# Rotary parts of queries and keys in a hybrid decoder layer: transposed on TensorE instead of by block transposes and placing DMAs

## The chip, the core and the metric

One core of a Trainium2 chip runs the whole layer. The metric is device time in microseconds, the median of several runs of one kernel. The engines are TensorE (PE, matrix products, results go to PSUM), VectorE (DVE), ScalarE (ACT), GpSimd (POOL) and SyncE (SP, which here issues nearly all DMAs). They run their own queues in program order and meet by semaphores.

## The reference, cut to what matters

```python
h = x @ w_in[l]                       # 512 tokens, 1024 wide
(qa, ka, va, ga, iq, ik, iw, c_q, c_kv, k_rope, gb) = _split_cols(h)
...
o_a = _dsa_branch(qa, ka, va, iq, ik, iw) * jax.nn.silu(ga)      # branch A: top-128 of the keys
# branch B: latent attention, 8 heads of 64 + 32
q = (_rmsnorm(c_q, q_norm_g) @ w_uq).reshape(B, S, B_HEADS, B_NOPE_DIM + B_ROPE_DIM)
q_nope, q_pe = q[..., :B_NOPE_DIM], _rope(q[..., B_NOPE_DIM:], pos)
k_pe = _rope(k_rope[:, :, None, :], pos)[:, :, 0, :]             # one key part for all heads
s = (einsum('bthd,bshd->bhts', qn, k_nope) + einsum('bthr,bsr->bhts', qp, k_pe)) * scale
...
out = jnp.concatenate([o_a, o_b], axis=-1) @ w_out[l]
x = _layernorm(DEEPNORM_ALPHA * x + out, ln_g[l], ln_b[l])
```

## The kernel before

All of it is one straight program. PE first multiplies x by the columns of w_in (groups of 512 columns, three products each for the high and low halves of the numbers), until about 159 us. Then come the small products of branch B: `qpe_tok` (the rotary part of the queries, tokens on partitions, 4 tiles of 128 tokens by 8 heads x 32), the 64-wide parts of `qbT` and `kbT` (head dimension on partitions, 512 tokens on the free axis), and `vb`. After these runs a loop over 64 units `u`: 8 heads for each of four query tiles of 128 tokens, branch A for u = 0 to 31 and branch B for u = 32 to 63. Query tiles are taken from the last, so the number of keys is 512 for u = 0 to 7, 384 for 8 to 15, then 256 and 128, and the same again for branch B.

In step u, PE computes the scores of u (L1310 and L1313, for branch B L1320), the transposes of the probabilities of u - 2 (L1355, `T_LAG`), and the value products of u - 4 (L1371, `PV_LAG`). DVE masks the scores and takes the row minimum (L951). ACT copies the transposed probabilities of u - 2 out of PSUM (L708) and computes the exponential of u (L688). At u = 12 and 13 DVE also normalises (L967, L968) and gates (L977) the first query tile. POOL, beside the loop, splits w_out into high and low parts (L511, L515): four of its eight row blocks come by `w_raw`, the others by `wo_early` and then `wo_raw_b`. After step 18 PE transposes a gated tile (L1400), and ACT copies it over the place where `wo_early` was, once all high parts of w_out are made.

The scores of branch B need `qbT` and `kbT` with all 96 rows: 64 rows by PE, and 32 rotary rows (partitions 64 to 95) that have to be turned from tokens on partitions to features on partitions. POOL rotates `qpe_tok` (L489 to L493, until about 172 us), DVE the key part `kpe_tok` (long before). Before the change the turning is done in two parts. DVE transposes blocks of 32x32 within their place: `kpe_blk` (L880) once, `qpe_blk` in four pieces (`qpe_blocks`, L939) at u = 3 to 6 (`PET_AT = 3`). Then SP issues four DMAs for each, one for each group of 32 partitions (`place`, L386), which carry the blocks, 32 elements at a stretch, to rows 64 to 95 of `kbT` (head 0) and of `qbT`. One more DMA (L403) copies the key rows of head 0 to the other seven heads.

SP works its list in order: the kaT_swap copies (L381, needed by the first scores, L1313), the four key placements, three loads of w_out to `w_raw` (L365), the key broadcast, two `wo_early` loads, a wait for `qpe_blocked`, the load of w_out block 0 (it goes to the place where `qpe_tok` lies), the four query placements, two more `wo_early` loads (each waits for a cast on POOL), and then a wait for the scores of u = 31 ahead of `wo_raw_b`. In front of unit 32, PE waits for `kpe_copied` and `qpe_placed`.

PSUM has 8 banks of 512 f32 columns. Banks 0 to 3 (`acc`) hold the products ahead of the loop; in the loop banks 2 and 3 are `ps_y`, idle until the output products at u = 34. `acc_ready` counts fills of these banks in order, `acc_read[i]` counts by twos what was read of bank i.

Of the kernel before, what the change touches and what calls it, by code (L numbers as in the profile page):

```python
# [6 lines left out]
P = 128  # L7
SEQ, D_MODEL = 512, 1024
TT = SEQ // P
# [5 lines left out]
B_HEADS, NOPE, ROPE_D, V_DIM = 8, 64, 32, 64  # L15
# [12 lines left out]
def build(nc, x, xT, positions, freqs, w_in, q_norm_g, w_uq, kv_norm_g, w_ukv, w_out, ln_g, ln_b, out):  # L28
# [93 lines left out]
    def sb(name, kib, shape, dt=f32):  # L122
        return nc.alloc_sbuf_tensor_at(name, shape, dt, offset=base + int(kib * 1024))
# [23 lines left out]
    qpe_blk = sb("qpe_blk", 94, [P, B_HEADS, TT, ROPE_D])  # L147
# [38 lines left out]
    kpe_blk = sb("kpe_blk", 204.5, [P, TT, ROPE_D])  # L186
    SQ = 32
# [23 lines left out]
    with ExitStack() as ctx:  # L211
# [14 lines left out]
        kaT_swapped, stored = sem("kaT_swapped"), sem("stored")  # L226
        kpe_blocked, qpe_blocked = sem("kpe_blocked"), sem("qpe_blocked")
        kpe_placed, kpe_copied, qpe_placed = sem("kpe_placed"), sem("kpe_copied"), sem("qpe_placed")
# [17 lines left out]
        qpe_rotated = sem("qpe_rotated")  # L246
# [33 lines left out]

        def seen(n):
            return 2 * (n // 4)
# [4 lines left out]
        ACC_LAST = [last_seen(range(A_END), b) for b in range(4)]  # L287
# [64 lines left out]
        def _(sp):  # L352
# [30 lines left out]
            def place(a, dst, blk, done):  # L383


                sp.dma_start(dst.rearrange("p h (m a t) -> p (h m) a t", a=P // SQ, t=SQ)[:, :, a, :],  # L386
                             blk[SQ * a:SQ * (a + 1)]).then_inc(done, 16)

            sp.wait_ge(kpe_blocked, 1)
            for a in range(P // SQ):  # L390
                place(a, kbT[NOPE:B_QK, 0:1, :], kpe_blk, kpe_placed)

# [9 lines left out]
            sp.wait_ge(kpe_placed, 16 * P // SQ)  # L402
            sp.dma_start(kbT[NOPE:B_QK, 1:B_HEADS, :],  # L403
                         kbT[NOPE:B_QK, 0:1, :].broadcast_to([ROPE_D, B_HEADS - 1, SEQ])).then_inc(kpe_copied, 16)
            for k in (4, 5):
                load_early(k)
            sp.wait_ge(qpe_blocked, TT)
            load(C_OUT // 2)
            for a in range(P // SQ):
                place(a, qbT[NOPE:B_QK, :, :], qpe_blk[:, :, :, :].rearrange("p h m t -> p (h m) t"), qpe_placed)  # L410
            for k in (6, 7):
                load_early(k)
# [139 lines left out]
        def _(act):  # L552
# [18 lines left out]
            def evac_group(g):  # L571
                dst = {G_IDX: idx_tok, G_LAT: lat_tok, G_Q: q_tok, G_K: k_tok, G_V: va}.get(g, gate)
                off = A_WIDTH if g == G_GB else 0
                n = GROUPS[g][1]
                if g == G_GA:

                    act.wait_ge(relu_used, (TT - 1) * IDX_HEADS)
                    act.wait_ge(kpe_blocked, 1)
                    act.wait_ge(side_ready, F_LAT + QL_T + 1)
                if g == G_LAT:  # L580
                    for m in range(TT):
                        act.wait_ge(side_ready, m + 1)
                        act.activation(dst[:, m, 0:n], side[:, m, 0:n], ACT.Copy).then_inc(side_read[m], 2)
                    return
                for m in range(TT):
                    act.wait_ge(acc_ready, TT * ACC_GROUP[g] + m + 1)
                    act.activation(dst[:, m, off:off + n], acc[:, m, 0:n],
                                   ACT.Silu if g in (G_GA, G_GB) else ACT.Copy).then_inc(acc_read[m], 2)
# [95 lines left out]
            act.activation(unused, minus_half[:, 0:1], ACT.Exp)  # L684
            def exp_unit(u):
                N = unit(u)[3]
                act.wait_ge(masked_ready, u + 1)
                act.activation(probs[:, u % NPROBS, 0:N], probs[:, u % NPROBS, 0:N], ACT.Exp, bias=neg_max[:, u % 8:u % 8 + 1],  # L688
                               scale=-1.0, accum_out=row_sum[:, u:u + 1]).then_inc(probs_ready, 1)
# [53 lines left out]
            for u in range(NU + T_LAG):  # L743
# [12 lines left out]
                if 0 < i < TT and j == OT_AT + 2:  # L756
                    copy_oT_hi(i - 1, 1)
                if u == VB_EARLY:
                    vb_high(0)
# [12 lines left out]
        def _(dve):  # L772
# [101 lines left out]
            for m in range(TT):  # L874
                for j, (a, b) in enumerate(((0, Q_LORA), (Q_LORA, Q_LORA + KV_LORA))):
# [4 lines left out]
            V.transpose(kpe_blk[:, :, :].rearrange("p m t -> p (m t)"),  # L880
                        kpe_tok[:, :, :].rearrange("p m d -> p (m d)")).then_inc(kpe_blocked, 1)
# [54 lines left out]
            def qpe_blocks(m):  # L936

                dve.wait_ge(qpe_rotated, 2 * TT)
                V.transpose(qpe_blk[:, :, m, :], qpe_tok[:, m, :].rearrange("p (h d) -> p h d", d=ROPE_D)).then_inc(qpe_blocked, 1)  # L939
# [115 lines left out]
            for u in range(NU):  # L1055
# [19 lines left out]
                if PET_AT <= u < PET_AT + TT:  # L1075
                    qpe_blocks(u - PET_AT)
# [41 lines left out]
        def _(pe):  # L1118
# [178 lines left out]
            def scores(u):  # L1297
# [16 lines left out]
                else:  # L1314
                    if u == NU_A:
                        for p in range(4):
                            pe.wait_ge(acc_read[p], ACC_LAST[p])
                        pe.wait_ge(kpe_copied, 16)
                        pe.wait_ge(qpe_placed, 16 * P // SQ)
# [6 lines left out]
            for p in range(4):  # L1326
# [3 lines left out]
                                     (w_lo[:, s, cols], latT_hi[:, QL_T, :])), True, True).then_inc(acc_ready, 1)  # L1330
            for m in range(TT):
# [102 lines left out]
            for u in range(NU + PV_LAG):  # L1434
# [4 lines left out]
                if u - PV_LAG >= 0:  # L1439
                    outputs(u - PV_LAG)  # L1440
                i, j = divmod(u - NU_A, HEADS)
# [26 lines left out]
PET_AT = 3  # L1468
# [45 lines left out]
```

## Time and profile before

| | us |
|---|---|
| median of 3 runs | 302.81 |
| lowest, highest | 302.24, 303.14 |
| the profiled execution | 303.14 |
| its span in the trace | 301.3 |

Of the span, PE is busy 97%, PE's weight loads 84%, DVE 77%, POOL 57%, ACT 56%. The profile's busy time counts each instruction from start to end. PE's matmuls overlap (an instruction of 128 columns is listed with about 0.27 us, while the next starts after 0.11), so PE's pace is read from the distances of the starts, not from the durations. Idle time is listed with what ended it; idle time of an engine that others don't wait for costs nothing.

### The profile page before, as it was taken

The numbers are of one execution on the slowest core, as the hardware profiler recorded it, in microseconds if no ns is written. First come the engines' busy times: TensorE is split into PE (matmuls) and PEld (weight loads), VectorE is DVE, ScalarE is ACT, GpSimd is POOL, SyncE is SP. The second block draws the span as 40 slices with busy tenths as digits, with TensorE's granted clock in tenths as the row PEclk, the third lists the DMA queues.
The fourth block names the chain that finished last, engine by engine and source line by source line (L and its number), as shares of the span: only waits on it lengthen the run. The fifth ranks groups of instructions, "written<-read, shape, count | busy, mean of one in ns | idle before, by whom it ended". The sixth has DMA issues, their size and how long they took to land.

```text
span 301.3 us, 5146 instructions
## 1 busy us (share of the span) xinstructions
PE 292.1 (97%) x1634; PEld 251.9 (84%) x1634; DVE 230.9 (77%) x525; ACT 167.4 (56%) x405; POOL 171.3 (57%) x197
## 2 busy tenths in 40 slices
PE   8899999999999999999999999999999999999990
PEld 8899988888888888888888789999677788888890
DVE  2798987878999999997043653664998868977785
ACT  4764444585152262374358787788877786553200
POOL 5698957302999995635326788530494261817211
PEclk9999999999999999999999999999999999999997
DMA  7965552200244425320055577300950000030411
GB/s 238 324 185 166 156 163 71 70 2 0 76 136 139 138 77 141 100 70 2 0 139 147 215 197 175 110 2 23 347 191 0 2 0 2 36 107 0 141 70 70
DMA packets 19546, 31.84 MB, mean 106 GB/s; under 512 B 6496, under 2 KB 9056, under 8 KB 19520
## 3 DMA queue, kind: packets, MB, share of 16 engines
q1 hardware_dynamic: 19088, 31.35, 34.5%
q8 instruction: 13, 0.21, 0.3%
q10 hardware_dynamic: 432, 0.18, 0.3%
q14 instruction: 13, 0.11, 0.1%
HBM read 26.28 MB, written 2.10 MB: 94 GB/s over the span
## 4 chain that ended last, share of the span: by engine, by line
PE 93%; DMA 2%; DVE 2%; ACT 1%; issue 1%; SPq 0%; DVEq 0%; ACTq 0%
PE ps L1124 49%; PE ps L1427 15%; PE ps L1355 6%; PE ps L1371 5%; PE ps L1320 5%; PE ps L1386 3%; PE ps L1310 2%; DMA w_raw<-in_w_in 2%; PE ps L1313 2%; PE ps L1221 1%; PE ps L1139 1%; PE ps L1240 1%; PE ps L1400 1%; PE ps L1211 1%; DVE y_last L1038 0%
## 5 line engine op out<-in xcount | busy, mean ns | idle before, releaser
L470 POOL TENSOR_TENSOR w_lo<-w_raw,w_hi 128x512 fp32r<-128x512 f32 (+3 forms) x62 | 81.1, 1332 | 32.1 <-ACT w_hi L569 32.0
L1124 PE MATMUL ps<-w_hi,x_lo 128*128 128x512 f32 (+2 forms) x224 | 82.5, 371 | 0.0
L1124 PE MATMUL ps<-w_lo,x_hi 128*128 128x512 f32 (+2 forms) x224 | 82.5, 371 | 0.0
L569 ACT ACTIVATE w_hi<-w_raw 128x512 fp32r<-128x512 f32 (+3 forms) x62 | 35.9, 590 | 71.2 <-PE ps L1124 63.1
L1124 PE MATMUL ps<-w_hi,x_hi 128*128 128x512 f32 (+1 forms) x188 | 73.1, 389 | 0.0
L1124 PEld LDWEIGHTS ps<-w_hi,x_lo 128*128 128x128 f32 x224 | 42.1, 188 | 6.4
L1124 PEld LDWEIGHTS ps<-w_lo,x_hi 128*128 128x128 f32 x224 | 42.2, 188 | 5.9
L1427 PE MATMUL ps<-wo_hi,oT 128*128 128x512 f32 (+1 forms) x144 | 43.5, 372 | 0.0
L1124 PEld LDWEIGHTS ps<-w_hi,x_hi 128*128 128x128 f32 x188 | 35.3, 188 | 5.9
L688 ACT ACTIVATE probs<-probs,small 128x512 f32<-128x512 f32 (+3 forms) x64 | 35.7, 558 | 7.6 <-DVE small L951 7.1
L1355 PE MATMUL ps<-ident,probs 128*128 128x128 f32 x160 | 28.3, 274 | 0.4 <-ACT probs L688 0.2
L1427 PEld LDWEIGHTS ps<-wo_hi,oT 128*128 128x128 f32 x144 | 25.7, 189 | 3.3
L1355 PEld LDWEIGHTS ps<-ident,probs 128*128 128x128 f32 x160 | 20.1, 140 | 9.6 <-issue 5.0
L328 POOL TENSOR_TENSOR obT<-half_sum,crossed 64x128 f32<-64x128 f32 x30 | 15.7, 523 | 17.8 <-ACT crossed L741 16.0
L908 DVE MATCH_REPLACE8 score<-small,score 128x256 f32<-128x256 f32 (+2 forms) x48 | 25.6, 548 | 0.0
L951 DVE CUSTOM_DVE_ANT_0 probs<-ps,score 128x512 f32<-128x512 f32 (+2 forms) x24 | 13.3, 556 | 15.1 <-PE ps L1313 15.1
L905 DVE MAX8 small<-score 128x8 f32<-128x256 f32 (+2 forms) x48 | 23.6, 550 | 0.0
L951 DVE CUSTOM_DVE_ANT_0 probs<-ps,causal 128x128 f32<-128x128 f32 (+3 forms) x40 | 17.7, 444 | 6.8 <-PE ps L1313 3.3
L1320 PE MATMUL ps<-kbT,qbT 96*128 96x512 f32 (+3 forms) x64 | 22.7, 435 | 0.0
L1371 PE MATMUL ps<-va,probsT 128*128 128x64 f32 x160 | 21.4, 264 | 0.0
L1371 PEld LDWEIGHTS ps<-va,probsT 128*128 128x128 f32 x160 | 20.5, 193 | 0.6 <-issue 0.6
L982 DVE TENSOR_TENSOR probsT_b<-ps,probsT_b 128x512 fp32r<-128x512 f32 (+3 forms) x32 | 15.6, 488 | 5.0 <-ACT probsT_b L708 4.6
(161 smaller groups left out, 555.7 us busy)
## 6 DMA issues: line engine op xcount, KB each, us to landing
w_raw<-in_w_in SPq DMA_DIRECT2D x20, 512.0 KB, 3.6
kaT_swap<-kaT SPq DMA_DIRECT2D x8, 256.0 KB, 3.7
w_raw<-in_w_out SPq DMA_DIRECT2D x4, 512.0 KB, 4.0
wo_early<-in_w_out SPq DMA_DIRECT2D x4, 512.0 KB, 5.4
wo_raw_b<-in_w_out SPq DMA_DIRECT2D x4, 512.0 KB, 5.2
x_res<-in_x SPq DMA_DIRECT2D x4, 512.0 KB, 7.4
x_raw<-in_xT SPq DMA_DIRECT2D x3, 512.0 KB, 7.9
out_y<-y SPq DMA_DIRECT2D x6, 256.0 KB, 2.2
```

Of the source, the lines that this page charges most:

```text
L328: eng.tensor_tensor(obT[rows, g % 4], half_sum[rows, g % 2, a], crossed[rows, g % 2], ALU.add).then_inc(pair_merged, 1)
L470: pool.tensor_tensor(w_lo[:, s, 0:n], w_raw[:, s, 0:n], w_hi[:, s, 0:n], ALU.subtract).then_inc(w_lo_ready, 1)
L569: act.activation(dst, w_raw[:, s, 0:n], ACT.Copy).then_inc(w_hi_ready, 1)
L688: act.activation(probs[:, u % NPROBS, 0:N], probs[:, u % NPROBS, 0:N], ACT.Exp, bias=neg_max[:, u % 8:u % 8 + 1], scale=-1.0, accum_out=ro ...
L905: step(V.max(top8[:, 8 * j:8 * j + 8], sc))
L908: step(V.match_replace(out=sc, in_to_replace=top8[:, 8 * j:8 * j + 8], in_values=sc, imm_value=TAKEN))
L951: V.tensor_tensor_reduce(out=probs[:, u % NPROBS, 0:N], in0=ps_s[:, u % 2, 0:N], in1=bias, scale=-scale, scalar=3.0e38, op0=ALU.add, op1=A ...
L1124: ins = mm(dst, a, b, start=start and j == 0, stop=stop and j == len(pairs) - 1)
L1320: ins = mm(ps_s[:, b, 0:N], qbT[:, h, t], kbT[:, h, 0:N], start=True, stop=True)
L1355: ins = nc.tensor.transpose(bank[:, j * P:(j + 1) * P], probs[:, u % NPROBS, j * P:(j + 1) * P], ident[:, :])
L1371: ins = mm(ps_o[:, v % 2, h * A_DIM:(h + 1) * A_DIM], probsT[:, u % 3, j * P:(j + 1) * P], va[:, j, h * A_DIM:(h + 1) * A_DIM], start=(j = ...
L1427: ins = mm(out_ps(i, b), oT[i % 2][:, o, k, :], w[:, wcols], start=first, stop=final)
```

## The change

The block transposes and the placing DMAs are taken out. PE transposes `qpe_tok` against the identity into the two banks `ps_y`: `qpe_transposes`, eight transposes, two groups of four heads, at the end of step u = 8 (`PET_AT` is now 8). The result has 128 partitions, 4 heads x 32, and 512 tokens. Four pieces of 32 partitions of each kind are then copied to rows 64 to 95 of `qbT`: heads 0, 1, 4, 5 by ACT and heads 2, 3, 6, 7 by DVE, one piece on each engine in each of the steps u = 9 to 12. At the end of u = 14 PE transposes `kpe_tok` (four transposes with 32 result partitions, `kpe_transposes`) into bank 2, and ACT copies it to `kbT`, head 0, at u = 15. The broadcast to the other heads stays a DMA, now last in SP's list before the wait for u = 31. In the diff the first `evac_qpeT` is ACT's, the second DVE's. The load of w_out block 0 waits until PE's second group of query transposes is done, instead of for DVE's.

```diff
-            for a in range(P // SQ):
-                place(a, kbT[NOPE:B_QK, 0:1, :], kpe_blk, kpe_placed)
...
             sp.wait_ge(acc_ready, A_END)
-            sp.wait_ge(kpe_placed, 16 * P // SQ)
+            for k in (4, 5):
+                load_early(k)
+            sp.wait_ge(acc_ready, A_END + 2)
+            load(C_OUT // 2)
+            for k in (6, 7):
+                load_early(k)
+            sp.wait_ge(acc_read[2], ACC_LAST[2])
             sp.dma_start(kbT[NOPE:B_QK, 1:B_HEADS, :],
                          kbT[NOPE:B_QK, 0:1, :].broadcast_to([ROPE_D, B_HEADS - 1, SEQ])).then_inc(kpe_copied, 16)
-            for k in (4, 5):
-                load_early(k)
-            sp.wait_ge(qpe_blocked, TT)
-            load(C_OUT // 2)
-            for a in range(P // SQ):
-                place(a, qbT[NOPE:B_QK, :, :], qpe_blk[:, :, :, :].rearrange("p h m t -> p (h m) t"), qpe_placed)
-            for k in (6, 7):
-                load_early(k)
...
+            def evac_qpeT(j):
+
+                quad, r = divmod(j, 2)
+                act.wait_ge(acc_ready, A_END + quad + 1)
+                ins = act.activation(qbT[NOPE:B_QK, 4 * quad + r, :], ps_y[32 * r:32 * r + 32, quad], ACT.Copy)
+                if r == 1:
+                    ins.then_inc(acc_read[2 + quad], 1)
...
+                if 0 <= u - PET_AT - 1 < 4:
+                    evac_qpeT(u - PET_AT - 1)
+                if u == PET_AT + 7:
+                    act.wait_ge(acc_ready, A_END + 3)
+                    act.activation(kbT[NOPE:B_QK, 0, :], ps_y[0:ROPE_D, 0], ACT.Copy).then_inc(acc_read[2], 2)
...
-            V.transpose(kpe_blk[:, :, :].rearrange("p m t -> p (m t)"),
-                        kpe_tok[:, :, :].rearrange("p m d -> p (m d)")).then_inc(kpe_blocked, 1)
+            dve.sem_inc(kpe_rotated, 1)
...
-            def qpe_blocks(m):
-
-                dve.wait_ge(qpe_rotated, 2 * TT)
-                V.transpose(qpe_blk[:, :, m, :], qpe_tok[:, m, :].rearrange("p (h d) -> p h d", d=ROPE_D)).then_inc(qpe_blocked, 1)
+            def evac_qpeT(j):
+
+                quad, r = divmod(j, 2)
+                dve.wait_ge(acc_ready, A_END + quad + 1)
+                ins = V.tensor_copy(qbT[NOPE:B_QK, 4 * quad + 2 + r, :], ps_y[64 + 32 * r:96 + 32 * r, quad])
+                if r == 1:
+                    ins.then_inc(acc_read[2 + quad], 1)
...
-                        pe.wait_ge(qpe_placed, 16 * P // SQ)
...
+            def qpe_transposes():
+
+                pe.wait_ge(qpe_rotated, 2 * TT)
+                for quad in range(2):
+                    pe.wait_ge(acc_read[2 + quad], seen(A_QPET + quad))
+                    for m in range(TT):
+                        ins = nc.tensor.transpose(ps_y[:, quad, m * P:(m + 1) * P], qpe_tok[:, m, quad * P:(quad + 1) * P], ident[:, :])
+                    ins.then_inc(acc_ready, 1)
+
+            def kpe_transposes():
+                pe.wait_ge(kpe_rotated, 1)
+                pe.wait_ge(acc_read[2], seen(A_KPET))
+                for m in range(TT):
+                    ins = nc.tensor.transpose(ps_y[0:ROPE_D, 0, m * P:(m + 1) * P], kpe_tok[:, m, :], ident[:, :])
+                ins.then_inc(acc_ready, 1)
...
+                if u == PET_AT:
+                    qpe_transposes()
+                if u == PET_AT + 6:
+                    kpe_transposes()
...
-PET_AT = 3
+PET_AT = 8
```

On PE, between the value products of step 8 and the scores of step 9, `ps<-kaT,qaT` are scores and `ps<-va,probsT` value products. Before:

```order
L1371 MATMUL ps<-va,probsT 128x64 [waits probsT_copied]
L1371 MATMUL ps<-va,probsT 128x64 x3
L1310 MATMUL ps<-kaT,qaT 128x384 [waits masked_ready]
L1313 MATMUL ps<-kaT_swap,qaT 128x384
L1355 MATMUL ps<-ident,probs 128x128 [waits probs_ready,probsT_copied]
```

and with the change (line numbers are those of the changed file):

```order
L1387 MATMUL ps<-va,probsT 128x64 [waits probsT_copied]
L1387 MATMUL ps<-va,probsT 128x64 x3
L1338 MATMUL ps<-ident,qpe_tok 128x128 [waits acc_read2,qpe_rotated]
L1338 MATMUL ps<-ident,qpe_tok 128x128 x3
L1338 MATMUL ps<-ident,qpe_tok 128x128 [waits acc_read3]
L1338 MATMUL ps<-ident,qpe_tok 128x128 x3
L1312 MATMUL ps<-kaT,qaT 128x384 [waits masked_ready]
L1315 MATMUL ps<-kaT_swap,qaT 128x384
```

Eight transposes stand between the two steps; four more (`ps<-ident,kpe_tok 32x128`) stand in the same way behind step 14. Nothing else of PE's order moves.

On DVE, around step 12, `probs,small<-ps,score` is the mask and `o_norm` the normalised tile of branch A. Before:

```order
L951 ISA probs,small<-ps,score 128x384 [waits transposed,scores_ready]
L951 ISA small 128x1
L967 RECIPROCAL small<-small 128x8 [waits pv_done]
L968 TENSOR_TENSOR o_norm<-ps,small 128x512 [waits dve_step]
L951 ISA probs,small<-ps,score 128x384 [waits transposed,scores_ready]
```

and with the change:

```order
L953 ISA probs,small<-ps,score 128x384 [waits transposed,scores_ready]
L953 ISA small 128x1
L969 RECIPROCAL small<-small 128x8 [waits pv_done]
L970 TENSOR_TENSOR o_norm<-ps,small 128x512 [waits dve_step]
L938 COPY qbT<-ps 32x512 [waits acc_ready]
L953 ISA probs,small<-ps,score 128x384 [waits transposed,scores_ready]
```

The fourth of DVE's copies stands behind the normalisation of step 12 and ahead of the mask of step 13.

On SP, after the kaT_swap copies, before:

```order
L386 DMA kbT<-kpe_blk 32x4x32 [waits kpe_blocked]
L386 DMA kbT<-kpe_blk 32x4x32 x3
L365 DMA w_raw<-in_w_out 128x1024 [waits w_lo_ready] x3
L403 DMA kbT<-kbT 32x7x512 [waits kpe_placed,acc_ready]
L397 DMA wo_early<-in_w_out 128x1024 x2
L365 DMA w_raw<-in_w_out 128x1024 [waits w_lo_ready,qpe_blocked]
L386 DMA qbT<-qpe_blk 32x32x32 x4
L397 DMA wo_early<-in_w_out 128x1024 [waits wo_hi_ready] x2
L415 DMA wo_raw_b<-in_w_out 128x1024 [waits scores_ready]
```

and with the change:

```order
L362 DMA w_raw<-in_w_out 128x1024 [waits w_lo_ready] x3
L384 DMA wo_early<-in_w_out 128x1024 [waits acc_ready]
L384 DMA wo_early<-in_w_out 128x1024
L362 DMA w_raw<-in_w_out 128x1024 [waits w_lo_ready,acc_ready]
L384 DMA wo_early<-in_w_out 128x1024 [waits wo_hi_ready] x2
L396 DMA kbT<-kbT 32x7x512 [waits acc_read2]
L400 DMA wo_raw_b<-in_w_out 128x1024 [waits scores_ready]
```

The placements are gone, the w_out loads stand right behind the kaT_swap copies, and the broadcast of the key rows stands behind all `wo_early` loads.

## Rows read from the trace of the kernel before

**Rows 1.** The page: busy us, share of span, instructions; PE's granted clock in tenths.

```profile
PE 292.1 (97%) x1634; PEld 251.9 (84%) x1634; DVE 230.9 (77%) x525; ACT 167.4 (56%) x405; POOL 171.3 (57%) x197
...
PEclk9999999999999999999999999999999999999997
```

**Rows 2.** The page: the chain that ended last, shares by engine.

```profile
PE 93%; DMA 2%; DVE 2%; ACT 1%; issue 1%; SPq 0%; DVEq 0%; ACTq 0%
```

**Rows 3.** Waits, 173 to 209.5: engine, line waited for, total us, times, longest us.

```profile
DVE probs L951 <- PE ps L1313: 18.4, 25, 2.4
...
PEld ps L1355 <- issue: 0.5, 1, 0.5
PEld ps L1355 <- DVE oT L338: 0.3, 1, 0.3
```

**Rows 4.** PE in order of time: start us, us, what, count [idle before].

```profile
175.40 0.47 PE L1310 MATMUL ps<-kaT,qaT 128*128 128x512 f32 x1
...
177.49 0.48 PE L1310 MATMUL ps<-kaT,qaT 128*128 128x512 f32 x1
...
181.09 0.48 PE L1310 MATMUL ps<-kaT,qaT 128*128 128x512 f32 x1
...
182.07 1.00 PE L1371 MATMUL ps<-va,probsT 128*128 128x64 f32 x8
```

**Rows 5.** The chain in order of time: start us, us, what.

```profile
110.24 1.31 PE ps L1228 x12
```

**Rows 6.** PE in order of time, around the transposes of a gated tile.

```profile
198.43 0.61 PE L1400 MATMUL ps<-ident,gate 128*128 128x128 f32 x4
198.80 0.36 PE L1310 MATMUL ps<-kaT,qaT 128*128 128x256 f32 x1
```

**Rows 7.** PE in order of time, the first scores of unit 32.

```profile
209.45 1.10 PE L1320 MATMUL ps<-kbT,qbT 96*128 96x512 f32 x2
```

**Rows 8.** DVE in order of time, u = 3 to 5.

```profile
175.86 0.44 DVE L939 STREAM_TRANSPOSE qpe_blk<-qpe_tok 128x256 f32<-128x256 f32 x1
176.22 0.65 DVE L951 CUSTOM_DVE_ANT_0 probs<-ps,score 128x512 f32<-128x512 f32 x1
...
178.24 0.69 DVE L951 CUSTOM_DVE_ANT_0 probs<-ps,score 128x512 f32<-128x512 f32 x1 [0.99 <-PE ps L1313]
```

**Rows 9.** The tile qbT: duration ns min/median/max, first and last start us.

```profile
L959 DVE COPY qbT<-ps x4: 692/694/694, 163.2 to 167.3; 64x512 f32<-64x512 f32 x4
L694 ACT ACTIVATE qbT<-ps x4: 574/593/596, 163.7 to 167.3; 64x512 f32<-64x512 f32 x4
```

**Rows 10.** In order of time, steps 12 to 15, of DVE, ACT and PE.

```profile
190.75 0.69 DVE L968 TENSOR_TENSOR o_norm<-ps,small 128x512 f32<-128x512 f32 x1
...
191.71 0.49 ACT L708 ACTIVATE probsT<-ps 128x384 f32<-128x384 f32 x1 [0.27 <-PE ps L1355]
192.10 0.61 ACT L688 ACTIVATE probs<-probs,small 128x384 f32<-128x384 f32 x1
...
193.89 0.49 PE L1355 MATMUL ps<-ident,probs 128*128 128x128 f32 x3
```

**Rows 11.** SP in order of time; PE's first use of kaT_swap, and its landing.

```profile
162.27 3.89 SPq L386 DMA_DIRECT2D kbT<-kpe_blk  x4
...
181.50 3.92 SPq L386 DMA_DIRECT2D qbT<-qpe_blk  x4
...
167.34 0.39 PE L1313 MATMUL ps<-kaT_swap,qaT 128*128 128x512 f32 x1
...
DMA to landing us min/median/max: 3.1/3.7/4.5
```

**Rows 12.** POOL in order of time, its work on w_out and behind it.

```profile
190.32 1.18 POOL L511 CAST wo_hi<-wo_early 128x512 fp32r<-128x512 f32 x2 [2.87 <-DMA wo_early<-in_w_out]
...
202.46 1.39 POOL L518 TENSOR_TENSOR vb_parts<-vb,vb_parts 128x512 fp32r<-128x512 f32 x1 [4.99 <-ACT vb_parts L732]
```

**Rows 13.** The key broadcast, L403: us from issue to landing.

```profile
DMA to landing us min/median/max: 4.5/4.5/4.5
```

More of the change, by code:

```diff
@@ L146, in build @@
     tmp = sb("tmp", 94, [P, 2, BANK])
-    qpe_blk = sb("qpe_blk", 94, [P, B_HEADS, TT, ROPE_D])
     y = sb("y", 94, [P, D_MODEL])
@@ L185, in build @@
     crossed = sb("crossed", 204.5, [P, 2, P])
-    kpe_blk = sb("kpe_blk", 204.5, [P, TT, ROPE_D])
-    SQ = 32
     def wo_lo(k, half):
@@ L225, in build @@
         xres_loaded = [sem(f"xres_loaded{i}") for i in range(2)]
-        kaT_swapped, stored = sem("kaT_swapped"), sem("stored")
-        kpe_blocked, qpe_blocked = sem("kpe_blocked"), sem("qpe_blocked")
-        kpe_placed, kpe_copied, qpe_placed = sem("kpe_placed"), sem("kpe_copied"), sem("qpe_placed")
+        kaT_swapped, kpe_copied, stored = sem("kaT_swapped"), sem("kpe_copied"), sem("stored")
         const_ready = sem("const_ready")
@@ L245, in build @@
         lat_normed, lat_hi_ready = sem("lat_normed"), sem("lat_hi_ready")
-        qpe_rotated = sem("qpe_rotated")
+        kpe_rotated, qpe_rotated = sem("kpe_rotated"), sem("qpe_rotated")
         q_step, q_rotated = sem("q_step"), sem("q_rotated")
@@ L279, in build @@
         A_END = A_VB + TT
+        A_QPET, A_KPET = A_END + 2, A_END + 6
         def seen(n):
@@ L285, in last_seen @@
             return seen([n for n in fills if n % 4 == bank][-1]) + 2
-        ACC_LAST = [last_seen(range(A_END), b) for b in range(4)]
+        ACC_LAST = [last_seen([*range(A_END), A_QPET, A_QPET + 1, A_KPET], b) for b in range(4)]
         SIDE_LAST = [last_seen(range(F_END), b) for b in range(4)]
@@ L382, in _ @@
                                  kaT[A_DIM * (1 - a):A_DIM * (2 - a), h:h + 2, :].bitcast(f32)).then_inc(kaT_swapped, 16)
[L383 to L389, printed above, removed]
-            for a in range(P // SQ):
-                place(a, kbT[NOPE:B_QK, 0:1, :], kpe_blk, kpe_placed)
             def load_early(k):
@@ L577, in evac_group @@
                     act.wait_ge(relu_used, (TT - 1) * IDX_HEADS)
-                    act.wait_ge(kpe_blocked, 1)
+                    act.wait_ge(kpe_rotated, 1)
                     act.wait_ge(side_ready, F_LAT + QL_T + 1)
@@ L1074, in _ @@
                     row_sums(v - 1)
-                if PET_AT <= u < PET_AT + TT:
-                    qpe_blocks(u - PET_AT)
+                if 0 <= u - PET_AT - 1 < 4:
+                    evac_qpeT(u - PET_AT - 1)
                 if u == O_FIRST + T_LAG + 1:
```

## The prediction

> **What bounds the kernel now.** I read the share of busy time first, then the chain of work that ended last, then the waits of the stretch that the change touches, then its instructions in order of time. TensorE (PE) is busy for 292.1 of 301.3 us, the next engine, VectorE (DVE), for 77% [rows 1]. The chain agrees: 93% of it is PE's [rows 2]. What matters is the stretch of the first attention loop (units u = 0 to 31, about 174 to 209 us), because all new PE work goes there. In its list of waits the long one is DVE's for PE: 18.4 us until scores (L1313) are done; PE's own weight loads wait 0.5 us for the sequencer and 0.3 for DVE [rows 3]. The instructions in order of time show a fixed beat: the steps of u = 5 and u = 7 start at 177.49 and 181.09, twice 1.80 us apart, with PE's groups end to end [rows 4]. So here PE's time is the kernel's time, and its granted clock is full in every slice but the last [rows 1].
>
> **PE, added.** Twelve transposes: eight of the query tile at the end of step u = 8 and four of the key tile at the end of u = 14. The chain has twelve transposes of the first form (128x128 f32, against the identity) as one piece, 1.31 us for L1228, that is 0.109 us each [rows 5]. A second reading is a group of four that stands between the loop's own groups, as the new ones will: L1400 starts at 198.43 and the scores behind it at 198.80, 0.37 us for four [rows 6]. Twelve cost 3 x 0.37 = 1.11 by this and 1.31 by the other. I take 1.3, since in a run of eight only the last overlaps what follows. Nothing of PE's is removed: the waits for placed queries and copied keys stood in front of unit 32, whose first scores start at 209.45 without idle time before them [rows 7], so these waits cost nothing.
>
> **DVE and ACT.** DVE loses one block transpose early in the run and four of 0.44 us in u = 3 to 6 [rows 8]. Their cover is DVE's waiting: behind the second of them the mask of u = 5 starts at 178.24 after 0.99 us of idle time that PE's scores end, and those of u = 6 and 7 start after idle time too [rows 8]. Only the mask at 176.22 starts as a block transpose ends (175.86 + 0.44), and PE's scores for it, begun at 175.40 [rows 4], end hardly earlier. I count the removal at nothing. Added are four copies on DVE and five on ACT, 32x512 out of PSUM. The nearest rows are the 64x512 copies: 0.69 us on DVE, 0.59 on ACT [rows 9]. Whether half the partitions is cheaper no row shows; between nothing and these values I take the whole. On ACT the step of u = 12 has 0.27 us of waiting for PE [rows 10], and a 512-column copy holds the engine about 0.5 us (one of 384 columns lets the next start after 0.39, 191.71 to 192.10 [rows 10]). ACT falls behind by about 0.2 us there and catches up in the next step. On DVE the tightest place is u = 12, where the normalisation already stands, 0.69 us at 190.75 [rows 10] and 0.2 for the reciprocals ahead of it: mask 0.6, normalisation 0.9, copy 0.65 make 2.15 us in a beat of 1.35, and the mask of u = 13 comes some 0.8 us late. From there it goes to the exponential on ACT (0.6 us, at 192.10 in this trace: 0.7 with its sum) and to PE's transposes of u = 13, two steps on, at 193.89 [rows 10]: 193.89 - 192.10 - 0.7 leaves 1.1 us, and the key transposes, which stand ahead of them, add 0.4. So a lateness of 0.8 is covered. If that cover is gone, it costs up to 0.8 us.
>
> **SP and its queue.** The eight placing DMAs go. They held SP for 3.89 us from 162.27 and for 3.92 us from 181.50 [rows 11]. What is queued behind them moves: three loads of w_out from 166.2 to about 162.3, and that of k = 0 from 181.1 to about 185.5, since it now waits for PE's eight transposes. The three loads then share the queue with the end of the kaT_swap copies, whose data PE needs at 167.34; the last of these was issued by 162.27 and they land in 3.7 us, 4.5 at most [rows 11], so 0.6 us is left at worst, and what stands behind them in the same queue should not overtake them. On POOL the cast of wo_early at 190.32 waited 2.87 us for its data, behind the placing traffic. With the load of k = 0 in its place it comes about as early, and after its last w_out piece POOL idles 4.99 us, until 202.46 [rows 12], so it is done at 197.5; ACT needs the high parts, made before that, only behind L1400's group at 198.43 [rows 6]. A slip of 1 us is covered twice. The key broadcast moves from 173.9 to behind PE's key transposes: step 15's own transposes start at 193.89 [rows 10], so step 14 ends about 193.4 + 0.9 + 0.4 = 194.7, ACT copies by about 197, the DMA takes 0.6 to issue and 4.5 to land [rows 13], so 202. It is needed at 209.45 + 1.3 = 210.7: 8 us of cover. Behind it are the wo_raw_b loads, which wait for unit 31 anyway.
>
> **A rule against this.** The Trainium skill, VectorE: DVE Perf Modes, section Rules for kernel authors, calls the DVE transpose the fastest for 32x32 blocks and sends full 128x128 ones to TensorE. By it the old way is the cheap one; this trace does not contradict it, since the block transposes hid in DVE's idle time. It leaves the sum as it is: 0 for the old way, 1.3 for the new.
>
> **Sum.** Removed from the path 0, added 1.3 (PE), all else covered: the profiled execution took 303.14 us over a span of 301.3, so it would be 304.4. That execution was the slowest of the three shown; on the median of 302.81 I forecast 304.1.
>
> **Rivals.** (a) The four key transposes cost double. They write only 32 partitions, from a stationary tile of 32 columns, a form that no row of before has. An ordinary f32 product shows as two records (L1371: 8 records for the 4 products of a step) [rows 4]; if these four ran so, they would add 4 x 0.11 = 0.44, which gives 304.5. For it speaks the unusual form; against it only that all other transposes are single records. The Trainium skill, TensorEngine Tiling (Array Packing), section Restrictions, states that column tiling disables the transpose mode for FP32 input, which would make them just that. (b) The copies stall the loop at u = 12 to 14: +0.8 on top, 304.9. It decides when the mask of u = 13 is more than 1.1 us late. (c) PE's insertion fills waits of its own: the step at 175.40 takes 2.09 us for 1.80 [rows 4], and 0.3 is lost to DVE [rows 3], near 200 us. If both swallowed new work, +0.7 is left, 303.5, no change that can be measured. Against it: the first lies ahead of the new work, the second hangs on PE's own L1400. (d) Faster: the loop is in truth a round trip (scores, mask, exponential, transpose), PE's records only look dense, and taking 4 x 0.44 = 1.8 us off DVE shortens it while the transposes fill holes: 301.0. It decides if masks start where DVE gets free; in u = 4 to 7 three of four start after an idle gap, so hardly.
>
> **How the numbers follow.** Forecast (304.1) 0.62; (a) 0.15; (b) 0.07; (c) 0.12; (d) 0.04. A measurement of this kernel tells about 0.3% from no change, 0.9 us. The forecast lies 1.3 above the median, so with the spread of the three runs (302.24 to 303.14) about one in eight of its outcomes falls within 0.3%. Slower: 0.54 + 0.15 + 0.07 = 0.76; same: 0.08 + 0.12 = 0.20; faster 0.04. The range takes in (a), most of (b), the bounds of the transposes (1.1 to 1.75) and part of (c): 303.2 to 305.2.
>
> **What would show it.** PE busy up by about 1.3 us; twelve new transposes, the step of u = 8 about 0.85 us longer and that of u = 14 about 0.4; later steps of PE unchanged, the first scores of unit 32 near 210.7 with no wait for the key broadcast; the mask of u = 13 late, with no gap of PE at u = 15. The forecast is wrong if eight records stand for the key tile, if PE waits for ACT or DVE between u = 9 and 16, or if PE waits for kaT_swap near 167.

## The result and the profile after

| | before | after |
|---|---|---|
| median of the runs, us | 302.81 (5 runs) | 304.31 (5 runs) |
| lowest, highest | 302.24, 303.14 | 303.78, 304.45 |
| the profiled execution | 303.14 | 303.76 |
| its span | 301.3 | 302.0 |

The ratio is 1.0052, with an interval of 1.0040 to 1.0065: the change costs 1.5 us (1.2 to 2.0). The forecast was 304.1. Over all 14 executions on record the changed kernel took 303.76 to 305.00 us.

The two spans differ by 0.7 us only. The profiled execution of before was the slowest of its runs and that of after is below all five runs in the table, so the two spans show less of the difference than the medians do. Before anything is explained the span has to be cut at places that both kernels have. I take four: the first scores of u = 2, the first scores of unit 32, the start of SP's last store issues, and the end of the span. The first two stand in PE's list in order of time (start us, us, engine line, operation, count):

```profile
172.67 0.39 PE L1312 MATMUL ps<-kaT,qaT 128*128 128x512 f32 x1
...
209.64 1.10 PE L1321 MATMUL ps<-kbT,qbT 96*128 96x512 f32 x2
```

The same first row of the kernel before, whose second is in [rows 7]:

```profile
173.68 0.39 PE L1310 MATMUL ps<-kaT,qaT 128*128 128x512 f32 x1
```

And SP's list in order of time, its last row, before and then after:

```profile
298.00 1.31 SPq L424 DMA_DIRECT2D out_y<-y_last  x3
```

```profile
298.19 1.30 SPq L409 DMA_DIRECT2D out_y<-y_last  x3
```

| stretch | before | after | difference |
|---|---|---|---|
| start to scores of u = 2 | 173.68 | 172.67 | -1.01 |
| the loop, u = 2 to unit 32 | 35.77 | 36.97 | **+1.20** |
| unit 32 to SP's last store issues | 88.55 | 88.55 | 0.00 |
| from the end of these issues to the end of the span | 1.99 | 2.51 | **+0.52** |

(301.3 - 298.00 - 1.31 = 1.99; 302.0 - 298.19 - 1.30 = 2.51.) The sum is 0.7. The spans are printed to 0.1 us, so the last row is good to 0.1 us only; the packed trace gives 2.01 and 2.46 us, a difference of 0.45. The first stretch, ahead of all that the change touches on PE, differs from kernel to kernel: in those below it ends at 173.06 and 173.17 with the placing DMAs of before (e1, e5), at 172.95 to 173.00 without them (e2, e3, e4, e6, e9), and at 173.46 and 173.53 with tiny DMAs added to these (e8, e10). Of the 1.01 us here, 0.67 is in the first 20 us of the program, where PE is idle for 1.84 us before and 1.17 after. What stands out is that the loop has the forecast's term and the end of the program has one that nobody had on the list.

The page of the kernel after, first part (busy us, share of the span, instructions), against [rows 1]:

```profile
PE 292.9 (97%) x1646; PEld 252.9 (84%) x1646; DVE 232.2 (77%) x524; ACT 169.9 (56%) x410; POOL 172.0 (57%) x197
```

PE has exactly twelve records more. Its list in order of time shows where they stand, first the eight of the query tile and then the four of the key tile:

```profile
182.74 1.00 PE L1387 MATMUL ps<-va,probsT 128*128 128x64 f32 x8
183.58 1.04 PE L1338 MATMUL ps<-ident,qpe_tok 128*128 128x128 f32 x8
184.38 0.42 PE L1312 MATMUL ps<-kaT,qaT 128*128 128x384 f32 x1
...
193.30 0.60 PE L1345 MATMUL ps<-ident,kpe_tok 128*32 128x128 f32 x4
193.65 0.42 PE L1312 MATMUL ps<-kaT,qaT 128*128 128x384 f32 x1
193.91 0.34 PE L1315 MATMUL ps<-kaT_swap,qaT 128*128 128x384 f32 x1
194.09 0.49 PE L1371 MATMUL ps<-ident,probs 128*128 128x128 f32 x3
```

From start to start the eight take 0.80 us and the four 0.35, together 1.15 of the loop's 1.20; counted from scores to scores, the step of u = 8 is 0.83 us longer and that of u = 14 is 0.38 longer. The scores, transposes and value products behind them follow at their old distances: nothing absorbs the twelve and nothing stalls because of them. The waits of the loop (173 to 211 us: engine, line waited for, total us, times, longest us; PEld is PE's weight loads) answer to [rows 3]:

```profile
DVE probs L953 <- PE ps L1315: 17.7, 25, 2.5
...
PEld ps L1371 <- issue: 0.5, 1, 0.5
PEld ps L1371 <- DVE oT L335: 0.3, 1, 0.3
```

DVE waits 0.7 us less for PE, and PE's own waits are the old ones.

### The profile page after: what moved, and what is told of

Its sections match the earlier page's. It is cut to its first block, busy times and chain, and to the rows that moved or that the text cites. A ratio compares the mean times of both kernels' runs of the same rounds, so it can differ in the third digit from the quotient of the medians.

```text
span 302.0 us, 5169 instructions
## 1 busy us (share of the span) xinstructions
PE 292.9 (97%) x1646; PEld 252.9 (84%) x1646; DVE 232.2 (77%) x524; ACT 169.9 (56%) x410; POOL 172.0 (57%) x197
## 4 chain that ended last, share of the span: by engine, by line
PE 93%; DVE 2%; DMA 2%; ACT 1%; issue 1%; SPq 0%; DVEq 0%; ACTq 0%
PE ps L1126 49%; PE ps L1443 15%; PE ps L1371 6%; PE ps L1387 5%; PE ps L1321 5%; PE ps L1402 3%; PE ps L1312 2%; PE ps L1315 2%; DMA w_raw<-in_w_in 2%; PE ps L1223 1%; PE ps L1141 1%; PE ps L1242 1%; PE ps L1416 1%; PE ps L1213 1%; DVE y_last L1040 0%
```

## Experiments

The loop of each kernel is measured as above, from the first scores of u = 2 to those of unit 32, and "the end" is the stretch from the end of SP's last store issues to the end of the span. Kernels with a median were run several times, and their ratio is to the kernel before as it ran beside them (median 302.64 beside e1 and e3, 302.63 beside e5 to e8). The others were profiled once: e2 took 306.03 us, e4 305.86, e9 303.70, e10 304.29 and e11 304.74. Each end is good to about 0.05 us, since the spans are printed to 0.1.

| kernel | loop | end | median | ratio |
|---|---|---|---|---|
| before | 35.77 | 1.99 | 302.81 | |
| after | 36.97 | 2.51 | 304.31 | 1.0052 [1.0040, 1.0065] |
| e1: before + 12 transposes | 36.97 | 2.03 | 303.68 | 1.0033 [1.0021, 1.0045] |
| e2: eight copies twice | 38.95 | 2.41 | | |
| e3: query transposes twice | 37.85 | 2.42 | 304.92 | 1.0074 [1.0052, 1.0097] |
| e4: key transposes five times | 38.72 | 2.41 | | |
| e5: block transposes twice | 35.81 | 1.98 | 302.74 | 1.0007 [0.9995, 1.0020] |
| e6: key transposes at u = 4 | 36.76 | 2.49 | 304.06 | 1.0046 [1.0032, 1.0060] |
| e7: before with gaps closed | (see there) | 2.06 | 302.10 | 0.9981 [0.9972, 0.9990] |
| e8: 8 tiny DMAs on SP | 36.97 | 2.02 | 303.83 | 1.0042 [1.0028, 1.0056] |
| e9: 24 waits on SP | 36.99 | 2.11 | | |
| e10: 4 tiny DMAs on SP | 36.99 | 2.10 | | |
| e11: before + 8 tiny DMAs | 35.78 | 2.02 | | |

### e1: only the twelve transposes

The kernel before, with twelve transposes whose results nobody reads. No copies, and the block transposes and placing DMAs stay.

```diff
+                if u == 8:
+                    for quad in range(2):
+                        pe.wait_ge(acc_read[2 + quad], ACC_LAST[2 + quad])
+                        for m in range(TT):
+                            nc.tensor.transpose(ps_y[:, quad, m * P:(m + 1) * P], ident[:, :], ident[:, :])
+                if u == 14:
+                    for m in range(TT):
+                        nc.tensor.transpose(ps_y[0:ROPE_D, 0, m * P:(m + 1) * P], kpe_tok[:, m, :], ident[:, :])
```

> The kernel before, with its block transposes and placing DMAs kept, plus twelve transposes on PE at the same two places (eight behind step 8, four behind step 14) whose results nobody reads. Theory (only PE's added work counts, the removal is worth nothing): the loop from the first scores of u = 2 to those of u = 32 takes 36.97 us as in the changed kernel, against 35.77 before, and the median comes out at 304.1 to 304.3, level with the changed kernel. Rival (the old way cost something that the change gave back, or the copies cost something): the loop differs from 36.97 by more than 0.1 us.

The loop takes 36.97 us, to the hundredth what it takes in the changed kernel (173.06 to this row of PE's list in order of time):

```profile
210.03 1.10 PE L1320 MATMUL ps<-kbT,qbT 96*128 96x512 f32 x2
```

So the whole of the loop's +1.20 is the twelve transposes; the nine copies and the removed DVE and SP work together change nothing. But the ratio is 1.0033, that is +1.0 us (0.6 to 1.4), against 1.5 for the change, and the expected median, 304.1 to 304.3, was missed. What the changed kernel has beyond e1 in the profiles is its longer end, 2.51 us for 2.03.

### e3 and e4: what one transpose costs, of either kind

e3 does the eight query transposes twice, e4 the four key transposes five times; results are the same.

```diff
-                    for m in range(TT):
+                    for m in [*range(TT), *range(TT)]:
                         ins = nc.tensor.transpose(ps_y[:, quad, m * P:(m + 1) * P], qpe_tok[:, m, quad * P:(quad + 1) * P], ident[:, :])
...
-                for m in range(TT):
+                for m in [*range(TT)] * 5:
                     ins = nc.tensor.transpose(ps_y[0:ROPE_D, 0, m * P:(m + 1) * P], kpe_tok[:, m, :], ident[:, :])
```

> The changed kernel with the eight query transposes done twice (sixteen, into the same banks). Theory (each costs PE its full 0.109 us, nothing absorbs it): the loop grows by 0.87 us to 37.84, the median to about 305.2. Rival (part of the transposes hides in PE's own waits): less than 0.7 us.

> The changed kernel with the four key transposes (stationary tile of 32 columns, 32 result partitions) done five times over, sixteen more. Theory (each takes what a full one takes, 0.109 us): the loop grows by 16 x 0.109 = 1.74 us to 38.7. Rival (they run as ordinary f32 products, twice the time): 3.5 us, with two records each. A third possibility, since the weight load of 32 columns is shorter (97 ns against 140): under 1.7 us.

e3's loop is 0.88 us longer for eight more, e4's 1.75 us for sixteen more: 0.110 and 0.109 us each. (e3's median, 304.92, lies under the 305.2 that was expected, but its interval takes that in.) In e4's list of PE in order of time the twenty stand as twenty records:

```profile
193.61 2.35 PE L1345 MATMUL ps<-ident,kpe_tok 128*32 128x128 f32 x20
195.72 0.42 PE L1312 MATMUL ps<-kaT,qaT 128*128 128x384 f32 x1
```

Rival (a) needed two records for each. The tile kpe_tok of the changed kernel tells why the narrow form brings nothing either (duration ns min/median/max, first and last start):

```profile
L1345 PEld LDWEIGHTS ps<-ident,kpe_tok x4: 97/97/153, 193.2 to 193.5; 128*32 128x32 f32 x4
L1345 PE MATMUL ps<-ident,kpe_tok x4: 272/272/273, 193.3 to 193.6; 128*32 128x128 f32 x4
```

The weight load of 32 columns takes 97 ns where one of 128 columns takes 140, but the load runs beside the product before it, and the product moves 128 columns in both cases. That these moved columns set the price is likely but not shown: no run varied them.

### e2: every copy twice

The changed kernel with eight more copies out of PSUM into scratch, one more beside each of the query copies.

```diff
+                act.activation(tmp[32 * quad:32 * quad + 32, r, :], ps_y[32 * r:32 * r + 32, quad], ACT.Copy)
                 ins = act.activation(qbT[NOPE:B_QK, 4 * quad + r, :], ps_y[32 * r:32 * r + 32, quad], ACT.Copy)
...
+                V.tensor_copy(tmp[64 + 32 * quad:96 + 32 * quad, r, :], ps_y[64 + 32 * r:96 + 32 * r, quad])
                 ins = V.tensor_copy(qbT[NOPE:B_QK, 4 * quad + 2 + r, :], ps_y[64 + 32 * r:96 + 32 * r, quad])
```

> The changed kernel with each of the eight query copies out of PSUM done twice, the second time to a spare place. Theory (the copies are covered with up to 1.1 us of room at the mask of u = 13): one more copy on DVE at u = 12 makes that mask about 0.65 us later still, about 1.3 us late in all, and ACT falls behind by 0.5 us in each of four steps; the cover is just used up, so the loop grows by 0.2 to 1.0 us over 36.97. Rival (copies have no part in the pace of PE at all): the loop stays at 36.97.

The loop is 38.95 us, 1.98 more than the changed kernel's. That is more than I had expected (0.2 to 1.0), and the engine that PE waits for is not DVE. PE's list in order of time (in brackets the idle time before, and what ended it):

```profile
193.88 0.52 PE L1373 MATMUL ps<-ident,probs 128*128 128x128 f32 x3 [0.76 <-ACT probs L683]
...
196.20 0.52 PE L1373 MATMUL ps<-ident,probs 128*128 128x128 f32 x3 [0.41 <-ACT probs L683]
```

and ACT's, with no idle time in two whole steps:

```profile
191.46 0.59 ACT L674 ACTIVATE tmp<-ps 32x512 f32<-32x512 f32 x1
192.06 0.58 ACT L675 ACTIVATE qbT<-ps 32x512 f32<-32x512 f32 x1
192.65 0.49 ACT L703 ACTIVATE probsT<-ps 128x384 f32<-128x384 f32 x1
193.04 0.60 ACT L683 ACTIVATE probs<-probs,small 128x384 f32<-128x384 f32 x1
193.54 0.19 ACT L683 ACTIVATION_READ_ACCUMULATOR probs<-probs,small 128x1 f32 x1
193.76 0.59 ACT L674 ACTIVATE tmp<-ps 32x512 f32<-32x512 f32 x1
```

One round of ACT is 193.76 - 191.46 = 2.30 us there, where PE's steps of the changed kernel take 1.69 to 1.57 us up to u = 11 and 1.35 from u = 12. DVE has no idle time either, but its mask of u = 13 is done at 194.60, and ACT comes to that exponential only at 195.36, behind its own copies. With one copy ACT's round is 1.7 us (190.10 to 191.81 in the changed kernel), which is already over the beat. That PE was not reached there, because only four such steps follow each other and the exponential is wanted two steps later, is my reading and was not tested apart. So the nine copies are free, but the change stands close to the edge: one more copy on each of the two engines in each of these four steps cost 1.98 us, more than the transposes do. What ACT's copies alone would cost was not run.

### e5: are the block transposes free?

The kernel before, each of DVE's four query block transposes done twice (the first into scratch).

```diff
+                V.transpose(qpe_blk2[:, :, m, :], qpe_tok[:, m, :].rearrange("p (h d) -> p h d", d=ROPE_D))
                 V.transpose(qpe_blk[:, :, m, :], qpe_tok[:, m, :].rearrange("p (h d) -> p h d", d=ROPE_D)).then_inc(qpe_blocked, 1)
```

> The kernel before with each of DVE's four block transposes of the query tile done twice, the second time to a spare place. Theory (DVE waits for PE in these steps, so its block transposes are free): the loop stays at 35.77, the median within 0.3% of before. Rival (the loop is a round trip and DVE's transposes are part of it): it grows by up to 1.8 us, and what the change took off DVE was worth as much.

The loop is 35.81 us for 35.77, and the ratio 1.0007 [0.9995, 1.0020]. (The single block transpose of the key part, long before the loop, was not doubled.) DVE's list in order of time shows the idle time that paid for it, ended by PE's scores:

```profile
178.35 0.44 DVE L940 STREAM_TRANSPOSE qpe_blk<-qpe_tok 128x256 f32<-128x256 f32 x1
178.71 0.40 DVE L941 STREAM_TRANSPOSE qpe_blk<-qpe_tok 128x256 f32<-128x256 f32 x1
179.53 0.69 DVE L953 CUSTOM_DVE_ANT_0 probs<-ps,score 128x512 f32<-128x512 f32 x1 [0.42 <-PE ps L1315]
```

Work that can be doubled at no cost is worth nothing when it is removed. That ends rival (d).

### e6: the key transposes in PE's gap

Rival (c) said that PE's gap in the step of u = 4 (2.09 us for 1.80) could take new work in. The change had put nothing there, so this kernel moves the four key transposes between the scores and the transposes of that step; counts and waits are renumbered for it.

```diff
+                if u == KPET_AT:
+                    kpe_transposes()
                 if 0 <= u - T_LAG < NU:
...
-                if u == PET_AT + 6:
-                    kpe_transposes()
...
+KPET_AT = 4
```

> The changed kernel with the four key transposes moved from behind step 14 to step 4, ahead of the transposes of u = 2, where PE waits about 0.3 us for ACT; ACT's copy of them goes to step 5. Theory (work put into a gap of PE costs only what is over the gap): the key transposes cost about 0.1 us instead of 0.37, the loop takes 36.7. Rival (what is put ahead shifts what PE waits for, so the gap stays): 36.97.

PE's list in order of time:

```profile
175.03 0.39 PE L1315 MATMUL ps<-kaT_swap,qaT 128*128 128x512 f32 x1
175.26 0.60 PE L1345 MATMUL ps<-ident,kpe_tok 128*32 128x128 f32 x4
175.69 0.60 PE L1371 MATMUL ps<-ident,probs 128*128 128x128 f32 x4
```

The step takes 2.22 us (174.72 to 176.94) for 2.09, and the loop 36.76 for 36.97. So 0.21 of the four transposes' 0.35 is swallowed and 0.14 is paid. The gap is a real hole, and the rival's mechanism is right; the change did not use it. The median, 304.06, is in line but its interval overlaps that of the change.

### e7: the kernel before with its gaps closed

The first tile's transposes (L1400) go to an idle bank of `ps_y` instead of taking a turn of the probabilities' two banks, and the scores and exponential of u = 2 come ahead of the products for `vb`.

```diff
+        def o_bank(i, b):
+            return ps_y[:, 0] if (i, b) == (0, 0) else ps_pT[:, slot_of[i, b] % 2]
...
+            exp_unit(2)
             for m in range(TT):
...
-                if 2 <= u < NU:
+                if 3 <= u < NU:
                     exp_unit(u)
...
+            scores(2)
             for m in range(TT):
...
+                elif slots[n - 2] == (0, 0):
+                    pe.wait_ge(probsT_copied, slots[n - 4] + 1)
...
+                if (i, b) == (0, 0):
+                    pe.wait_ge(acc_read[2], ACC_LAST[2])
+                    bank = o_bank(i, b)
```

> A variant of the kernel before, for the two gaps of PE in the loop: (1) the scores of u = 2 stand ahead of the four vb products, and ACT's exponential of u = 2 ahead of its four copies of vb, so that the transposes of u = 2 need not wait in step 4; (2) the transposes of the first gated tile go to bank 2, idle until u = 34, so that the transposes of u = 18 need not wait for DVE's low parts. Theory (PE's waits are all that is left to win here): 0.3 us from each, 0.6 in all from the first vb product to unit 32, the median at about 302.1 to 302.3. Rival (the waits move to the next step): within 0.2 us of before.

This one is faster than both kernels: 302.10 us, ratio 0.9981 [0.9972, 0.9990]. The median is as expected, but only one of the two gaps was closed, so the expectation's reason holds for half of it. PE's list in order of time near 200 us, before and then e7:

```profile
200.12 0.28 PE L1313 MATMUL ps<-kaT_swap,qaT 128*128 128x256 f32 x1
200.51 0.44 PE L1355 MATMUL ps<-ident,probs 128*128 128x128 f32 x2
```

```profile
199.56 0.28 PE L1317 MATMUL ps<-kaT_swap,qaT 128*128 128x256 f32 x1
199.68 0.38 PE L1362 MATMUL ps<-ident,probs 128*128 128x128 f32 x2
```

The distance falls from 0.39 to 0.12 us: this gap is closed. The other is not:

```profile
175.15 0.39 PE L1317 MATMUL ps<-kaT_swap,qaT 128*128 128x512 f32 x1
175.63 0.66 PE L1362 MATMUL ps<-ident,probs 128*128 128x128 f32 x4
```

0.48 us where a step without a gap has 0.23. Taking the exponential of u = 2 earlier put another wait in its place. The chain that ended last shows it in order of time (start us, us, what):

```profile
174.00 1.09 ACT vb L704 x2
175.09 0.50 ACT probsT L712
175.63 0.66 PE ps L1362 x4
```

PE now waits for ACT's copy of the transposed probabilities (L712), and that copy stands behind the four copies of `vb`, which the edit moved behind the exponential. From the transposes of u = 0 to unit 32 e7 takes 35.02 us (173.58 to 208.60) and the kernel before 35.31, so 0.29 of the gain of 0.6 (0.3 to 0.8) is this one gap. Where the rest comes from was not taken apart, and the interval reaches down to the 0.3 that is explained.

### e8 to e11: the end of the program

All kernels whose SP list is that of the kernel before end 1.98 to 2.06 us after the last store issues, those with the changed list (after, e2, e3, e4, e6) 2.41 to 2.51 us. The last stores themselves need 2.0 to 2.1 us from issue to landing in either kind, and no view of the profile shows an instruction in the stretch. The changed list has eight DMAs less. e8 puts eight tiny DMAs (16 partitions by 4 numbers, into an unused tile) into it, four behind the kaT_swap copies and four behind the load of w_out block 0.

```diff
+            def pads(a):
+                for j in range(4):
+                    sp.dma_start(pad[16 * (a + j):16 * (a + j + 1), :], positions[16 * j:16 * j + 16, :]).then_inc(padded, 16)
+
+            pads(0)
...
+            pads(4)
```

> The changed kernel with eight tiny DMAs on SP (16x4 elements each) where the eight placements stood, so that SP's list is as long as before. In the changed kernel and all kernels made from it the span ends 2.4 to 2.5 us after SP has issued the last store, in the kernel before and in the one made from it (twelve transposes added) 2.0. Theory (the 0.4 us behind the last store hang on the length of SP's list): the distance goes back to 2.0 us and the median to about 303.8. Rival (it hangs on the work of another engine, or is nothing but the chip): it stays at 2.4 and the median at 304.2. In both the loop stays at 36.97.

Span 302.3, last row of SP's list:

```profile
298.98 1.30 SPq L418 DMA_DIRECT2D out_y<-y_last  x3
```

The end is 2.02 us, and the loop still 36.97. Work that does nothing for the kernel makes its end 0.45 us shorter by the packed trace (2.46 to 2.01); the median goes from 304.31 to 303.83, which is in line (the two intervals overlap, so it is the profiles that show it). Is it the DMAs or the mere number of instructions? e9 has 24 waits more on a count that is long reached, and no DMA; e10 has only the first four tiny DMAs; e11 adds eight to the kernel before.

```diff
+            for _ in range(24):
+                sp.wait_ge(acc_ready, 1)
```

> The changed kernel with 24 waits more in SP's list (on a count that is long reached), and no DMA more. The stretch from the end of SP's last store issue to the end of the span is 2.5 us in the changed kernel and 2.0 in the padded one of the run before. If the number of instructions in SP's list decides it, 2.0 or another value than 2.5 here. If the number of DMAs decides it, 2.5 as in the changed kernel. The loop is 36.97 in both.

> The changed kernel with four tiny DMAs more on SP instead of eight. If the stretch behind the last store falls in proportion to what stands in the list, about 2.25 us; if it goes by steps (a block of instructions that is fetched or not), 2.5 or 2.0. The loop is 36.97 in both.

> The kernel before with eight tiny DMAs more on SP, whose stretch behind the last store is 2.0 us without them. If a longer list is always better, 1.5 us; if 2.0 is the floor, 2.0; if it depends on where the list happens to end, as likely 2.5. The loop is 35.8 in all.

The ends are 2.11, 2.10 and 2.02 us. e9's last row of SP's list, at a span of 301.9, needs no DMA to be short:

```profile
298.49 1.30 SPq L412 DMA_DIRECT2D out_y<-y_last  x3
```

So the longer list need not hold more DMAs; waits that cost nothing do as well. The effect is a step rather than a proportion (four DMAs are as good as eight), and no list that was tried ended in less than 2.0 us.

The packed trace has more of this end than its views. Once the last store has landed, SP runs a branch and then a drain, and behind that all engines end. From the end of the branch to the start of the drain pass 0.43 to 0.45 us in the five kernels with the long end (after, e2, e3, e4, e6) and 0.13 to 0.14 us in the eight others. This pause is 0.3 of the 0.45 us. Of the rest, 0.05 is the drain itself, and 0.08 is a later landing of the last store (1.68 us from the end of its issue, for 1.60), which e9 and e10 have too. The page also has DMA queues of the kind "instruction" (packets, MB, share); one of them differs, before and then after:

```profile
q14 instruction: 13, 0.11, 0.1%
```

```profile
q14 instruction: 12, 0.10, 0.1%
```

All five kernels with the long end have 0.10 MB in it and all eight others 0.11. Its last transfer of 8192 bytes starts 0.3 us behind the end of the span in the five, and 9 to 38 us ahead of it in the eight. So the long end goes with one block of instructions less that was brought in before the end, in all 13 traces. That SP pauses for instructions there fits this, but is not shown: no record ties the queue to SP, and in the five the transfer starts only when the pause is over.

e11 as a whole was slow (304.74), since it reached the loop late, at 175.22; only its end is used here.

## Why the prediction was right, step by step

- **PE is the bound, and twelve transposes cost 1.11 to 1.31 us.** Right. The loop grew by 1.20, and by the same in e1, which has the transposes alone. The chain's 0.109 us each [rows 5] was the exact price (e3, e4: 0.110 and 0.109). I had taken 1.31, the sum for twelve in a row; 0.80 + 0.35 = 1.15 shows start to start. The signs came as named, 0.83 us for the step of u = 8 and 0.38 for that of u = 14 (0.85 and 0.4 were said). PE's busy time rose by 0.8 us over the whole span (292.1 to 292.9) and not by 1.3: in the loop it rose by 1.20 (35.54 to 36.74), and ahead of it it fell by 0.34.
- **The removal is worth nothing.** Right for DVE (e5) and for the path through SP's placements (e1, which keeps them, has the same loop). Not wholly right for SP: see the last point.
- **Copies of 32 partitions.** I took the whole price of the 64-partition rows [rows 9]. The tile qbT of the changed kernel:

```profile
L938 DVE COPY qbT<-ps x4: 689/692/696, 185.6 to 191.3; 32x512 f32<-32x512 f32 x4
L674 ACT ACTIVATE qbT<-ps x4: 585/586/587, 186.7 to 191.8; 32x512 f32<-32x512 f32 x4
```

  692 and 586 ns, against 694 and 593 for 64 partitions. Half the partitions are no cheaper.
- **The mask of u = 13 comes late, covered (rival b).** Right in size, and covered. PE's scores for it (L1315) start at 190.83 and are listed to 191.17; DVE's and ACT's lists in order of time:

```profile
191.29 0.69 DVE L938 COPY qbT<-ps 32x512 f32<-32x512 f32 x1
192.02 0.56 DVE L953 CUSTOM_DVE_ANT_0 probs<-ps,score 128x384 f32<-128x384 f32 x1
```

```profile
191.81 0.59 ACT L674 ACTIVATE qbT<-ps 32x512 f32<-32x512 f32 x1
192.42 0.49 ACT L702 ACTIVATE probsT<-ps 128x384 f32<-128x384 f32 x1
192.81 0.60 ACT L682 ACTIVATE probs<-probs,small 128x384 f32<-128x384 f32 x1
```

  The mask is 0.85 us late (0.8 was said), and the transposes of u = 13 start at 194.09 with no gap ahead of them. But the step looked at the wrong engine. The exponential at 192.81 had its mask and sum at 192.58; it waited at least as much for ACT's own two copies. "ACT falls behind by about 0.2 us and catches up" was too light: ACT is over its beat in all four steps, and when the copies are doubled it is ACT that stops PE (e2).
- **Rival (a), key transposes double.** False: four single records, 0.35 us for four. The Trainium skill, TensorEngine Tiling (Array Packing), section Restrictions, states that column tiling disables the transpose mode for FP32 input, and the prediction took that to make two records of each. This transpose of f32 into 32 result partitions ran as one (e4: twenty records for twenty); whether it counts as column tiling no run shows.
- **Rival (c), gaps swallow the new work.** Its mechanism is true (e6: 0.21 us of 0.35), its place was not: the work stands elsewhere, and both gaps are there unchanged. It was rightly given little.
- **Rival (d), faster by relief of DVE.** False (e5).
- **SP and the broadcast.** The key broadcast was issued at 196.35 and took 0.73 and 4.6 us, so it landed about 201, 8 us ahead of use. POOL's cast of wo_early came at 189.71 (190.32 before [rows 12]). PE did not wait for kaT_swap, though with the loads right behind them these copies took up to 5.2 us to land, where the prediction reckoned with 4.5 at most: the last was issued at 160.6, and the first scores that use it start at 166.3.
- **What was missed.** The sum had no term for the end of the program. It is 0.45 us by the packed trace, and e8 to e10 show that it comes with the shorter SP list. So "removed from the path 0" was right for the loop and wrong for the end: the removal itself has a price there. That the forecast, 304.1, came near 304.31 is in part luck: it had 0.1 us too much for the loop and nothing for the end. The two terms together, 1.65, lie within the measured 1.5 (1.2 to 2.0). The changed kernels without tiny DMAs reach the loop 0.06 to 1.0 us earlier than before, e1 and e5 (see the first stretches above), but each was profiled once, so whether anything of that is due to the change is open.

## What to carry to other kernels

Where one engine is dense from end to end, price an added instruction by the distance between starts on that engine, and a removed one by what it hid: work that could be done twice without a change in time (e5) was not worth a single instruction of the dense engine. Look for the dense engine's few holes first; here they were worth 0.2 us to the moved transposes (e6), and closing one by a free PSUM bank is 0.29 us of the gain of the only kernel that beats both (e7, 302.10 us). When small differences matter, cut the span at places that both kernels share, the end of the program included, before a cause is named.

## What the runs showed of the hardware

- A transpose of f32 on PE, among other products at the full granted clock, cost 0.110 us with 128 result partitions (e3) and 0.109 with 32 (e4), although the weight load of the narrow one takes 97 ns instead of 140.
- A copy of 512 columns out of PSUM took the same time for 32 as for 64 partitions, 0.69 us on DVE and 0.59 on ACT (the tile qbT, after and before).
- The stretch behind the last store depended on SP's instruction list: 2.4 to 2.5 us in the changed kernel and its near kin, 2.0 to 2.1 with four or eight tiny DMAs or 24 idle waits more. In the long ones SP pauses for 0.43 to 0.45 us between its last branch and its drain (0.13 to 0.14 in the others), and the last block of the instruction queue q14 comes after the end of the span instead of 9 to 38 us ahead of it. Whether the step lies in the length of the list or in where it happens to end was not tested apart, nor where it lies between the changed list and four DMAs more.
